# First expert's rows gathered by one-hot products inside routing, its first two panels split there, and the router's rows as the stationary operand

## What is computed

```python
h = rms_norm(x, g_ffn)                                   # x: 1024 tokens x 1024
logits = xt @ w_router + b_router                        # xt = h as rows; 32 experts
top_logit, top_idx = lax.top_k(logits, 4); gates = softmax(top_logit)
xs = xt[tok_sorted]                                      # rows gathered expert by expert
gu = ragged_dot(xs, w_gate_up, group_sizes) + b_gate_up  # 1024 -> 2048 per expert
gate = min(gate, 7); lin = clip(lin, -7, 7)
act = (lin + 1) * (gate * sigmoid(1.702 * gate))
out = ragged_dot(act, w_down, group_sizes) + b_down      # 1024 -> 1024 per expert
y = sum over the 4 chosen experts of gate * out;  rms_norm(x + y, g_final)
```

## Time and profile before

| what | us |
| --- | --- |
| median of 3 runs | 2510.11 |
| lowest, highest | 2508.51, 2512.55 |
| the profiled execution, its own time | 2506.09 |
| its span, first to last instruction | 2504.5 |
| PE busy in it | 2425.9 (97%) |
| first instructions of the experts block | from 1164.2 |

### The profile page before, as it was taken

How to read it: one execution, slowest core, us unless ns; L and a number is a source line. 1 busy time by engine, 2 the same in 40 slices (tenths; PEclk the granted TensorE clock), 3 DMA queues, 4 the chain that set the end, 5 groups by cost and what they waited for, 6 DMA issues and landing times.

```text
span 2504.5 us, 41446 instructions
## 1 busy us (share of the span) xinstructions
PE 2425.9 (97%) x14271; PEld 1958.6 (78%) x14272; DVE 1496.6 (60%) x1483; ACT 1223.8 (49%) x1256; POOL 368.8 (15%) x384
## 2 busy tenths in 40 slices
PE   7999999999999999995999999999999999999997
PEld 6987777898888877994778777777777787777775
DVE  4311333332333324335789888788877898788977
ACT  6412344321111111144667766676756776667766
POOL 0000000000000000434112121212112211212120
PEclk9999999999999999997999999999999999999998
DMA  4134233323422222535899997999989998989998
GB/s 132 35 40 62 68 68 72 59 48 51 51 51 51 92 93 81 183 124 183 292 365 381 337 348 280 345 342 346 336 285 316 377 379 307 324 303 380 350 338 304
DMA packets 262381, 537.08 MB, mean 214 GB/s; under 512 B 28984, under 2 KB 79928, under 8 KB 261184
## 3 DMA queue, kind: packets, MB, share of 16 engines
q1 hardware_dynamic: 241280, 489.35, 58.9%
q0 software_dynamic: 21024, 46.65, 6.8%
HBM read 493.32 MB, written 42.63 MB: 214 GB/s over the span
## 4 chain that ended last, share of the span: by engine, by line
PE 51%; DVE 1%; issue 0%; ACT 0%; DMA 0%; POOL 0%; POOLq 0%; DVEq 0%; ACTq 0%
PE m_gate L2171 5%; PE m_gate L2167 5%; PE m_lin L2167 5%; PE m_gate L2169 5%; PE m_lin L2171 5%; PE m_lin L2169 5%; PE m_y L2167 5%; PE m_y L2171 5%; PE m_y L2169 5%; PE m_spill L2208 3%; PE m_spill L2220 2%; PE m_turn L2159 1%; PE m_gate L2177 1%; PE m_gate L2145 1%; PE m_lin L2145 1%; PE m_y L2177 1%
## 5 line engine op out<-in xcount | busy, mean ns | idle before, releaser
L1982 DVE TENSOR_TENSOR m_w_lo<-raw,m_w_hi 128x2048 fp32r<-128x2048 f32 x384 | 871.4, 2287 | 208.9 <-ACT m_w_hi L1851 207.2
L1851 ACT CAST m_w_hi<-raw 128x2048 fp32r<-128x2048 f32 x384 | 734.5, 1914 | 356.8 <-PE m_lin L2171 251.4
L107 PE MATMUL c_bank<-h_hi_r,ring_hi 128*128 128x512 f32 x640 | 252.2, 394 | 0.9 <-PEq L397 0.9
L109 PE MATMUL c_bank<-h_lo_r,ring_hi 128*128 128x512 f32 x640 | 249.7, 390 | 0.0
L110 PE MATMUL c_bank<-h_hi_r,ring_raw_r 128*128 128x512 f32 x640 | 249.4, 390 | 0.0
L148 ACT CAST ring_hi<-ring_raw 128x2048 fp32r<-128x2048 f32 x43 | 82.0, 1908 | 306.6 <-DMA ring_raw<-in_w_in 133.6
L2167 PE MATMUL m_gate<-m_w_hi,m_x_hi 128*128 128x512 f32 x512 | 218.1, 426 | 0.0
L2167 PE MATMUL m_y<-m_w_hi,m_a_hi 128*128 128x512 f32 x512 | 211.0, 412 | 1.8 <-DVE m_a_lo L2034 1.8
L2171 PE MATMUL m_gate<-m_w_hi,m_x_lo 128*128 128x512 f32 x512 | 200.8, 392 | 0.0
L2167 PE MATMUL m_lin<-m_w_hi,m_x_hi 128*128 128x512 f32 x512 | 200.4, 391 | 0.0
L2171 PE MATMUL m_y<-m_w_hi,m_a_lo 128*128 128x512 f32 x512 | 200.4, 391 | 0.0
(11 more groups left out here) (337 smaller groups left out, 4501.7 us busy)
## 6 DMA issues: line engine op xcount, KB each, us to landing
raw<-in_w_gate_up SPq DMA_DIRECT2D x512, 512.0 KB, 11.4
raw<-in_w_down SPq DMA_DIRECT2D x256, 512.0 KB, 12.5
ring_raw<-in_w_in SPq DMA_DIRECT2D x31, 1024.0 KB, 10.1
gates<-work POOLq DMA_DIRECT2D x32, 256.0 KB, 2.6
work<-gates SPq DMA_DIRECT2D x8, 1024.0 KB, 6.8
v<-in_x SPq DMA_DIRECT2D x8, 512.0 KB, 11.3
ring_raw<-in_w_branch_b SPq DMA_DIRECT2D x4, 1024.0 KB, 5.0
ring_raw<-in_w_branch_a SPq DMA_DIRECT2D x4, 1024.0 KB, 5.0
```

The lines of the kernel that those rows point to most:

```text
L107: pe.matmul(out, left_hi(k), right_hi(k), start=first and k == kts[0], stop=False, skip_group_check=True)
L109: pe.matmul(out, left_hi(k), right_lo(k), start=False, stop=False, skip_group_check=True)
L1851: act.copy(w_hi[:, p % WS].rearrange("p k b n -> p (k b n)"), raw[:, raw_slot(m)].rearrange("p k b n -> p (k b n)")).then_inc(signals.whi, 1)
L1982: dve.tensor_tensor(w_lo[:, p % WS].rearrange("p k b n -> p (k b n)"), raw[:, raw_slot(m)].rearrange("p k b n -> p (k b n)"), f32(w_hi[:, ...
```

## The change

Three things are changed together.

**Router.** logit takes the turned rows xT as stationary operand and the router's weights as moving operand (32 columns), so logits come out as tokens by experts. The copy of the logits and turn_back are gone.

**First expert's rows.** seats computes, for each token of a tile, a key (its seat in expert 0 plus one, or zero where expert 0 is not chosen) and from it sel, a 128x128 matrix with the token's norm factor in the column of its seat. first_rows(i) multiplies x2 of tile i by sel and adds over the 8 tiles in PSUM (turned[0]), which gives expert 0's first 128 rows already turned. ACT scales them by g_ffn into x_hi and DVE makes x_lo, all at the end of routing. The first list of slots, the first gather and x_turn(0) are gone, and the counts in later waits are lowered by one gather.

**First two panels.** Panels 0 and 1 are split at the end of routing into m_hi, whose memory the output product no longer needs; PE's products read them there (first_weights). Panels 2 and 3 are loaded before the last h_rows store, split at the start of the experts block. Panels 4 and 5 are loaded at its start, 6 and 7 after first_spill, 8 to 11 after panel 1's products. PE's turning of the spill rows and its register loads move behind panel 3. The waits for stores and scatters move from POOL to SP. b_raw shares memory with ht.

```diff
@@ output_and_route, sync
+                if i == TT - 1:
+                    for m in range(2, 4):
+                        load_panel(sp, w_gate_up, w_down, raw, signals.raw_loaded, m, 0)
                 sp.wait_ge(normed, i + 1)
                 sp.dma_start(h_rows[i * P:(i + 1) * P, :], ht[:, i % HT]).then_inc(stored[i % HT], 16)
-            for m in range(2, 4):
-                load_panel(sp, w_gate_up, w_down, raw, signals.raw_loaded, m, 0)
+            for s in range(HT):
+                sp.wait_ge(stored[s], 16 * len(range(s, TT, HT)))
             sp.wait_ge(finished, 16 * (TT + 2))
+            sp.wait_ge(sent, 16 * TT * TOP_K)
@@ scalar
-                move_low(i)
...
+            act.wait_ge(ready, 4 * TT)
+            for m in range(2):
+                act.wait_ge(signals.raw_loaded[raw_slot(m)], OPEN + 32)
+                act.copy(m_hi[:, 4 * m:4 * m + 2].rearrange("p k n -> p (k n)"),
+                         raw[:, raw_slot(m)].rearrange("p k b n -> p (k b n)")).then_inc(signals.whi, 1)
+            for k in range(KT):
+                act.wait_ge(signals.x_turned, OPEN + k // 4 + 1)
+                split = act.activation(x_hi[:, k], turned[0][:, k * P:(k + 1) * P], ACT.Copy, scale=g_col[:, k:k + 1])
@@ vector, in seats
+                dve.scalar_tensor_tensor(out=key[:, i:i + 1], in0=p_rank[:, E * i:E * i + 1], scalar=1.0,
+                                         in1=chosen[:, i, 0:1], op0=ALU.add, op1=ALU.mult).then_inc(keyed, 1)
...
+                dve.wait_ge(keyed, i + 1)
+                dve.tensor_scalar(sel[:, i], iota1[:, :], key[:, i:i + 1], stat[:, 2, i:i + 1],
+                                  ALU.is_equal, ALU.mult).then_inc(selected, 1)
@@ tensor
-                    mm = pe.matmul(p_low[0:E, 0:P], wr[:, k], xT[:, i % 2, k], start=(k == 0), stop=(k == KT - 1))
+                    mm = pe.matmul(p_logits[:, 0:E], xT[:, i % 2, k], wr[:, k], start=(k == 0), stop=(k == KT - 1))
...
+            def first_rows(i):
+                pe.wait_ge(selected, i + 1)
+                for k in range(KT):
+                    mm = pe.matmul(turned[0][:, k * P:(k + 1) * P], x2[:, i, k * P:(k + 1) * P], sel[:, i],
+                                   start=i == 0 and k % 4 == 0, stop=i == TT - 1, skip_group_check=True)
...
+            pe.wait_ge(moved, TT - 1)
+            first_rows(0)
             turn(TT - 1)
             rank(TT - 2)
             logit(TT - 1)
-            turn_back(TT - 1)
+            first_rows(1)
             rank(TT - 1)
@@ experts, sync
-            sp.wait_ge(signals.gathered[0], 16)
+            for m in range(4, 6):
+                load_panel(sp, w_gate_up, w_down, raw, signals.raw_loaded, m, 0)
             sp.wait_ge(signals.first_spill, 16)
-            for m in range(4, MP):
+            for m in range(6, GU):
+                load_panel(sp, w_gate_up, w_down, raw, signals.raw_loaded, m, 0)
+            sp.wait_ge(signals.panel_done, OPEN + 2)
+            for m in range(GU, MP):
                 load_panel(sp, w_gate_up, w_down, raw, signals.raw_loaded, m, 0)
@@ experts, tensor
-            x_turn(0)
-            first_second = about(pe, held, 0)[0]
...
             for m in range(4):
                 pe.wait_ge(signals.wlo, OPEN + m + 1)
-                gate_up(m, m + 6)
-                if m == 0:
-                    pe.wait_ge(signals.first_spill, 16)
-                    xs_turn(first_second)
...
+                gate_up(m, m, first_weights if m < 2 else None)
+            pe.wait_ge(signals.panel_done, OPEN + 4)
+            pe.sem_inc(signals.panel_done, 2)
+            last = last_super(pe)
+            held = registers(pe)
+            first_second = about(pe, held, 0)[0]
+            pe.wait_ge(signals.first_spill, 16)
+            xs_turn(first_second)
```

More of the change, by code:

```diff
@@ L1063, in output_and_route @@
 def output_and_route(nc, x, w_out, g_ffn, w_router, b_router, b_gate_up, b_down, w_gate_up, w_down, h_rows, y_rows,
-                     slot_rows, cst, x2, mix, m_hi, m_lo, ring, now, where, expert_f, b_split, raw, slot_in, xg, xs_g, signals):
+                     slot_rows, cst, x2, mix, m_hi, m_lo, ring, now, where, expert_f, b_split, raw, x_hi, x_lo, signals):
     with ExitStack() as ctx:
@@ L1214, in _ @@
             step(pool.memset(ones[:, :], 1.0))
+            step(pool.tensor_scalar(iota1[:, :], cst["iota"][:, :], 1.0, None, ALU.add))
             pool.sem_inc(constant, 1)
@@ L1498, in _ @@
             mm.then_inc(counted, 1)
+            first_rows(2)
             pe.wait_ge(split_up, 1)
@@ L1501, in _ @@
                 .then_inc(shared, 1)
+            first_rows(3)
+            first_rows(4)
             pe.wait_ge(split_up, 5)
-            pe.matmul(turned[0][:, 0:4 * W + 1], ones[:, :], terms[:, :], start=True, stop=True).then_inc(summed, 1)
+            pe.matmul(p_out[:, 0:4 * W + 1], ones[:, :], terms[:, :], start=True, stop=True).then_inc(summed, 1)
+            for i in range(5, TT):
+                first_rows(i)
 class Signals:
@@ L1556, in __init__, with experts @@
         self.added = [sem(f"added{x}") for x in range(2)]
-def experts(nc, w_gate_up, w_down, h_rows, y_rows, slot_rows, cst, now, where, expert_f, b_split, raw, slot_in,
-            xg, xs_g, signals, g_final, out):
+def experts(nc, w_gate_up, w_down, h_rows, y_rows, slot_rows, cst, now, where, expert_f, b_split, raw, w_first, x_hi,
+            x_lo, slot_in, xg, xs_g, signals, g_final, out):
     h_quarters = h_rows.rearrange("r (g c) -> (r g) c", g=NG)
@@ L1822, in _ @@
             between = spills_between(pool, ahead, last + 2)
[L1823 removed]
+            pool.wait_ge(signals.in_listed[0], 16 * last + 32)
             pool.sem_inc(signals.waits_met, 1)
@@ L1975, in _ @@
         def _(dve):
-            last = last_super(dve)
-            held = registers(dve)
             def split(m, p, at):
@@ L2119, in _ @@
             pick_expert(0, 0, signals.picked_gu)
-            for m in range(2):
-                split(m, m + 6, OPEN + m + 1)
-            for r in range(2):
-                x_split(r, 0)
+            last = last_super(dve)
+            held = registers(dve)
             for m in range(2, 4):
-                split(m, m + 6, OPEN + m + 1)
+                split(m, m, OPEN + m + 1)
             dve.wait_ge(signals.wlo, OPEN + 4)
@@ L2137, in _ @@
         def _(pe):
-            last = last_super(pe)
-            held = registers(pe)
             def x_turn(n):
@@ L2161, in a_turn, with split_weights, first_weights, products @@
                 tr.then_inc(signals.turned, 1)
-            def products(m, p, half, out, signal=None):
+            def split_weights(m, p, k, half):
+                return w_hi[:, p % WS, k, half], w_lo[:, p % WS, k, half]
+            def first_weights(m, p, k, half):
+                cols = slice(half * NW, (half + 1) * NW)
+                return w_first[:, 4 * m + k, cols], w_first[:, 4 * m + 2 + k, cols]
+            def products(m, p, half, out, signal=None, weights=None):
                 left_hi, left_lo = (a_hi, a_lo) if m >= GU else (x_hi, x_lo)
@@ L2183, in gate_up @@
                     bias(p_lin[j][:, :], 0, F + NW * j)
-                products(m, p, 0, p_gate[j][:, :], signals.gate_done if m % 4 == 3 else None)
-                products(m, p, 1, p_lin[j][:, :], signals.panel_done)
+                products(m, p, 0, p_gate[j][:, :], signals.gate_done if m % 4 == 3 else None, weights)
+                products(m, p, 1, p_lin[j][:, :], signals.panel_done, weights)
             def down(m, p):
```

111 lines of the change are left out of this document (50 added, 61 removed).

## The result

The kernel after took 2522.9 us (median of 5, 2521.3 to 2527.3) where the kernel before, measured beside it, took 2512.0 us: ratio 1.0051, 95% interval 1.0039 to 1.0062. The forecast was 2500.5 us, faster. It is wrong in its sign: the change costs 0.5%.

The account below looks back on a forecast made before the run. PE was taken to bound the kernel, busy 97% of the span. Terms -1.2 + 1.0 - 11.0 + 0.8 + 0.8 summed to -9.6 us, taking 2510.1 to 2500.5 us; 8-in-10 range 2495.5 to 2506.5 us.

Parts of the forecast that it names:

- I measure the change by that point; all after it is the same work: Point is panel 4's start, 29.5 us behind the barrier before; work after it was taken as unchanged.
- the length from panel 4 to the end: Named sign of a wrong prediction: gain given back after panel 4; before, this length was 1310.9 us.
- barrier to panel 4: From the barrier's release to panel 4's start: 18.5 us instead of 29.5, term -11.0 us (-9.5 to -12).
- late next: After the spill products, DVE's splits of panels 4 to 7 start later and PE waits: +0.8 us (0 to +1.5).
- rival 2: First expert's later panels come late, PE waits some 3 to 4 us: 2504 us, chance 0.13.
- the clock: PE rests about 3.0 us before the bias products; half the price of half clock taken: +0.8 us (0 to +2.7).
- Token tiles: Routing's token tiles: swapped logits operands save 0.17 us per tile over 7 tiles, -1.2 us (0 to -3.8).
- last tile to barrier: End of routing: first_rows, panel splits and scatters put the barrier later by +1.0 us (0 to +3).
- rival 1: Logits' weight load is hidden, loop gains 0.54 us a tile and clock stays full: 2497.1 us, chance 0.12.
- rival 4: Half clock inside first_rows after PE's breaks between 1146 and 1153, barrier 8.0 us later: 2511.7 us, chance 0.06.

Follow-up runs that it names:

- e1: The kernel after with 128 unused bytes set ahead of x_hi and x_lo, nothing else; 2501.6 us, ratio 0.9976 to before.
- e2: The kernel before with x_hi and x_lo moved 128 bytes further up, nothing else changed; 2520.0 us, ratio 1.0045 to before.
- m1: Separate kernel timing sections of 64 f32r products at different offsets of the loaded operand; 226.6 ns a product at 256 bytes, 232.5 ns at 128.
- a4: The kernel after with each value loaded from the plan passed through a maximum with 0; ratio 1.0068 to before.
- b3: The kernel before with each value loaded from the plan passed through a maximum with 0; ratio 1.0001 to before.
- e9: a4 with 128 unused bytes ahead of x_hi and x_lo; ratio 1.0011 to before.
- e6: e1 with the loads of panels 4 to 7 issued in routing, right behind those of panels 2 and 3; ratio 0.9989 to before.
- e11: e9 with the loads of panels 4 to 7 issued in routing, right behind those of panels 2 and 3; 2501.8 us, ratio 0.9974 to before.
- e4: The kernel after with the loads of panels 2 and 3 back behind the last h_rows store; 2514.0 us, ratio 1.0022 to before.
- e3: The kernel before with only the router's part of the change (router's rows as loaded operand, second turn and copy gone); ratio 1.0005 to before.
- a2: The kernel after, unchanged, measured again in another group; 2526.3 us, ratio 1.0046 to before.

## Why the prediction was wrong

**The step that failed** is the first: "I measure the change by that point; all after it is the same work." The work is the same, its spacing is not. The change allots x_hi and x_lo at the other end of memory, 128 bytes off the weights modulo 256, and 10.8 us are lost evenly over 31 rows of the plan, a term that my sum put at nothing because the work is the same. It is shown from both sides (e1, e2) and alone (m1). The text named the length from panel 4 to the end as what would show it wrong, and it did: 1310.9 became 1327.8.

It is not the only step. With waits on both sides, a4 against b3 (medians 16.0 us apart), the stretches of the table set beside the sum are:

| stretch | forecast | a4 less b3 |
| --- | --- | --- |
| routing | -0.2 | +3.9 |
| barrier to panel 4, clock with it | -10.2 | -10.1 |
| panel 4 to row 2 (late next) | +0.8 | +8.6 |
| row 2 to the end | 0 | +10.7 |
| sum | -9.6 | +13.1 |

**Late next (+0.8)** was mis-sized. Against before, and b3, from panel 4 to row 2 it is +3.1 us without waits in routing (e1) and +4.8 (e9) with them, +6.0 to +8.7 in the three profiles of the kernel after. It is rival 2's mechanism in a wider form: not only the panels come late but the lists and rows that queue behind them, and each break that follows can cost the clock. In e9 POOL waits 5.90 us for the list of the spill rows, in b3 2.45. e6 and e11 take this stretch back to 0.3 to 0.6 us above before.

**Barrier to panel 4 (-11.0, and +0.8 for the clock)**: from about 1164.0 in e1 to 1185.56 it is 21.6 us where 19.3 were forecast. Bias (0.5) and the break ahead of the spill products (2.9, from 1177.3 to 1180.19) came as reckoned. The clock did not: half clock behind the barrier cost some 1.4 us, and the clock fell a second time behind the break of 2.9 us, so that the spill products took 5.4 us and not 3.7. I priced one fall up to panel 4, and there are two in e1. That the row above fits in a4 is luck: there the clock stayed full from the barrier to panel 4, though PE had stood for 3.4 us, and I had taken half of the price of a fall.

**Token tiles (-1.2) and last tile to barrier (+1.0)** held where routing had no waits: tiles of 6.4 us, routing 1.6 us shorter than before in e1 and e4, the pick at 1164.13, first_rows at 1.9 us and full clock. e3, the router alone, needs 1.1 us less for routing than b3, but in another group and with a longer first wait (5.06 us against 3.46), so this only agrees with the term of 1.2. The logits stayed at 0.111 us each, so rival 1 is out.

**The waits in routing** were in no part of the text, since the profile of before had none. With them the clock falls to half inside first_rows in all six profiles of changed kernels, as rival 4 said, but not always at the same products: the last 48 instructions took 8.47 us after and 5.62 in e1, while in a2, a4, e6 and e9 they took 5.62 too and earlier ones ran at half. Its trigger was another than the one I named. In b3's group the changed kernel loses about 4 us of routing to b3 instead of winning 1.6. What these waits are is not settled: in all eight profiles that have them the first begins after the same product, the last of tile 3, whichever the kernel; POOL goes on issuing meanwhile. The four groups behind the first ran on four chips, none used twice, so nothing here tells a chip from a session.

So the change itself, without the accident of placement, is worth -0.24% (e1) in a group without waits and +0.11% (e9) in one with them; the forecast's -0.38% was in sight of the first, with placement none of it is left. In groups without waits e1 and e11 are faster than before by 0.24% and 0.26%; with waits only e6 is, by 0.11%. The kernel after itself was never measured in a group without waits.

## What to carry to other kernels

When a change moves a 4-byte tensor that PE loads for thousands of products with 512 moving columns, compare its byte offset with that of the moving operand, modulo 256, before and after; an even loss over untouched work is the sign, and 128 bytes of padding are the test. Transfers issued behind a barrier push back the small lists and gathers that queue behind them, and issued ahead of it they push back the last store: look at both. And take two profiles of the kernel before, on two chips, before building on its idle times.

## What the hardware showed that I had not expected

- Two f32r operands with 512 moving columns: 226.6 ns a product where both stand at the same offset modulo 256 bytes, 232.5 to 234 ns elsewhere, 229 ns at 192 bytes; no difference with 256 columns, where the weight load is busy all the time, and none in bf16 (216 ns at 0, 32, 64, 128 and 256 bytes).
- Nearly the same program has waits of 3 to 5 us in routing on some chips and none on others (before and b3, e1 and e9, e6 and e11 differ by the maximum alone), and the unchanged kernel before moves with them, 2508 to 2514 us. The cause is open.
- Behind a break of 3.15 us PE ran at half clock in e1 (PEclk 0.50 from 1164.48 to 1167.44), and behind one of 3.4 us at the same place in a2, a4 and e9 it did not. In e1 it fell again after each of two later stretches with shorter waits.
